# Hybrid decoder layer: token norms from the turned tokens by TensorE in place of loaded prompt rows, constant tables loaded in other places, page numbers read once per pair

## The reference, cut to what matters

```python
xn = rmsnorm(h, norm1)                       # h: (tokens, 1024), all f32
p = xn @ w_in                                # 3592 columns: q, k, v, conv inputs, z, gates
oa = diff_attention(q, k, v, paged cache)    # 4 heads
ob, state = gated_delta(conv(qkv_b), g, beta)
h = h + concat(norm(oa), norm(ob) * silu(z)) @ w_out
h = h + peer_ffn(rmsnorm(h, norm2))          # 128 of 16384 experts per token, gathered
rmsnorm(x, g) = x * rsqrt(mean(x * x) + 1e-6) * g
```

## Time and profile before

| | |
|---|---|
| median of 3 runs | 2050.31 us (2047.03 to 2055.94) |
| the profiled execution | 2046.96 us |
| its span, first to last instruction | 2045.1 us |
| TensorE busy | 1691.6 us (83%) |
| VectorE busy | 1335.3 us (65%) |
| ScalarE busy | 802.0 us (39%) |
| GpSimd busy | 785.1 us (38%) |
| moved by DMA | 758.91 MB, 371 GB/s over the span |

### The profile page before, as it was taken

The page is one execution under the profiler, slowest core; times in us unless marked ns, Lnnn a source line. Parts: engine busy times, 40 slices in busy tenths (PEclk is TensorE's granted clock), DMA queues, the critical chain, the costliest instruction groups (busy, mean ns, idle before and its releaser), DMA issues.

```text
span 2045.1 us, 20559 instructions
## 1 busy us (share of the span) xinstructions
PE 1691.6 (83%) x6211; PEld 853.0 (42%) x6211; DVE 1335.3 (65%) x3023; ACT 802.0 (39%) x2371; POOL 785.1 (38%) x670
## 2 busy tenths in 40 slices
PE   7697999988897878989787888978997657866777
PEld 2242464547453445445344544533563213522111
DVE  1344514344897657897665888775688967679544
ACT  1342322131645523563453346354344423333332
POOL 2111110111444444435444353534444555554442
PEclk9798999999999989999898999999999888987999
DMA  9999823226999999999999999999999999999997
GB/s 333 358 309 382 263 92 118 93 104 244 406 414 409 427 428 428 426 426 411 428 421 429 426 426 400 416 426 393 427 427 426 427 427 427 427 427 427 427 427 313
DMA packets 137015, 758.91 MB, mean 371 GB/s; under 512 B 15263, under 2 KB 24495, under 8 KB 60472
## 3 DMA queue, kind: packets, MB, share of 16 engines
q0 software_dynamic: 88448, 622.22, 73.4%
q1 hardware_dynamic: 44976, 128.07, 16.8%
q10 hardware_dynamic: 3480, 7.31, 1.0%
HBM read 741.56 MB, written 16.26 MB: 371 GB/s over the span
## 4 chain that ended last, share of the span: by engine, by line
PE 38%; DMA 30%; DVE 16%; ACT 7%; issue 4%; SPq 3%; POOL 2%; ACTq 0%; DVEq 0%; POOLq 0%
DMA sb_uv<-in_peer_uv,sb_eidx 27%; PE bank L2224 16%; PE bank L1827 8%; DVE sb_uv L1806 7%; PE bank L2151 3%; PE bank L2191 2%; DVE sb_hres L1780 2%; SPq L841 1%; POOL sb_uv L1006 1%; SPq L845 1%; ACT sb_diag L1384 1%; DMA sb_w<-in_w_sections 1%; PE bank L1941 1%; ACT sb_ew L1377 1%; PE bank L1953 1%
## 5 line engine op out<-in xcount | busy, mean ns | idle before, releaser
L2224 PE MATMUL bank<-sb_uv,sb_diag 128*128 128x512 f32 (+1 forms) x1860 | 943.2, 643 | 277.8 <-ACT sb_diag L1384 267.8
L1006 POOL DMA_INDIRECT sb_uv<-in_peer_uv,sb_eidx x576 | 704.1, 1222 | 829.8 <-PE bank L2224 646.4
L1806 DVE CUSTOM_DVE_ANT_0 sb_uv<-sb_uv,sb_xn 128x1024 f32<-128x1024 f32 x576 | 698.9, 1220 | 280.5 <-DMA sb_uv<-in_peer_uv,sb_eidx 277.6
L2224 PEld LDWEIGHTS bank<-sb_uv,sb_diag 128*128 128x128 f32 (+1 forms) x1860 | 333.8, 194 | 766.4 <-ACT sb_diag L1384 440.7
L1373 ACT ACTIVATE sb_gel<-sb_h 128x1 f32<-128x1 f32 x576 | 116.3, 202 | 753.5 <-DVE sb_h L1806 750.4
L1827 PE MATMUL bank<-sb_w,sb_xnT 128*128 128x512 f32 (+1 forms) x560 | 270.3, 626 | 24.7 <-DMA sb_w<-in_w_sections 11.7
L1384 ACT ACTIVATE sb_diag<-sb_stay,sb_ew 128x128 f32<-128x128 f32 (+1 forms) x465 | 183.2, 394 | 45.7 <-PE bank L2224 2.5
L1377 ACT ACTIVATE sb_ew<-sb_gel,sb_gate 128x1 f32<-128x1 f32 x576 | 169.7, 295 | 19.8
L1827 PEld LDWEIGHTS bank<-sb_w,sb_xnT 128*128 128x128 f32 (+1 forms) x560 | 100.6, 190 | 149.8 <-issue 122.6
L1780 DVE SCALAR_TENSOR_TENSOR sb_hres<-sb_uv,sb_ew,sb_hres 128x1024 f32<-128x1024 f32 x111 | 142.2, 1281 | 0.1
L2191 PEld LDWEIGHTS bank<-sb_rT,sb_zone 128*128 128x128 f32 x832 | 99.3, 193 | 15.7 <-issue 15.3
(11 more groups left out here) (352 smaller groups left out, 1593.2 us busy)
## 6 DMA issues: line engine op xcount, KB each, us to landing
sb_zone<-in_w_route SPq DMA_DIRECT2D x11, 2304.0 KB, 11.8
sb_w<-in_w_sections SPq DMA_DIRECT2D x40, 512.0 KB, 7.3
sb_zone<-in_w_mixer SPq DMA_DIRECT2D x8, 2048.0 KB, 15.6
sb_uv<-in_peer_uv,sb_eidx POOLq DMA_INDIRECT x576, 14.0
sb_sS<-in_cache_kT SPq DMA_DIRECT2D x32, 256.0 KB, 7.3
sb_zone<-in_cache_kT SPq DMA_DIRECT2D x32, 256.0 KB, 7.2
sb_held<-in_cache_v SPq DMA_DIRECT2D x32, 256.0 KB, 7.0
sb_zone<-in_cache_v SPq DMA_DIRECT2D x32, 256.0 KB, 5.9
```

Source lines behind the costliest of these rows:

```text
L1006: nc.gpsimd.indirect_dma_start(uv[:, m % RING, :], None, i["peer_uv"], bass.IndirectOffsetOnAxis(ap=eidx[:, t % 2, n:n + 1], axis=0)).then ...
L1806: nc.vector.tensor_tensor_reduce(out=uv[:, m % RING, 0:D], in0=uv[:, m % RING, 0:D], in1=xn2[:, t % 2, :], scale=1.0, scalar=0.0, op0=ALU. ...
L2224: ins = nc.tensor.matmul(bank[half][0:rows, :], lhsT=G["diag"][:, d % DIAGS, 0:rows], rhs=uv[:, m % RING, D + 512 * half:D + 512 * half + ...
```

## The change

Five things are done together.

1. The rows of the four prompt tiles are not loaded in the front. ScalarE squares the *turned* tokens of tiles 0 to 3 from `xnT` into the same borrowed buffers, without a sum. `square_sums(n)` lets TensorE sum over the features: eight matmuls of 128x128 squares with one column of -0.5, into column n of bank 7. `x_mean` reads that column. VectorE's gain multiply of a tile now waits for its square (`s_xsq`). Tile `PT` keeps its rows.
2. `SUMMED`, the due times of squares, sums, means and powers, goes from (20.5, 60, 66, 72, 77) to (20.5, 35, 50, 57, 65).
3. `s_tables` is split. `s_early` counts `w_ba` and the early table, now due at 49 in place of 54 and 59; `s_stay` counts the rest of the stay table, now due at 110 in place of 56, and `gain2T`, whose 4 KB load goes from GpSimd to SP.
4. The values of a pair use the page numbers that SP read for its keys.
5. Pieces 22 and 23 (the last two of the third conv section's first use) have a due time 4.5 earlier.

```diff
-SUMMED = (20.5, 60, 66, 72, 77)
+SUMMED = (20.5, 35, 50, 57, 65)
...
                 def x_loads():
-                    for n, t in enumerate(ORDER):
-                        yield early_at((1.0, 42, 48, 53, 58)[n])
-                        if t < PT:
-                            sp.dma_start(xin[n], i["x_prompt"][0, 128 * t:128 * t + 128, :]).then_inc(s_x[n], 16)
...
+                    yield early_at(1.0)
+                    sp.dma_start(xin[0][0:NSAMP], i["x_sample"].rearrange("b s d -> (b s) d")).then_inc(s_x, 16)
+                    sp.dma_start(xin[0][MROW:LAST], i["meta_tokens"]).then_inc(s_x, 16)
...
-                    yield early_at(54)
-                    sp.dma_start(F["wba"][:, :, :], i["w_ba"]).then_inc(s_tables, 16)
-                    yield early_at(56)
-                    sp.dma_start(stay[:, 128:], stay_table[:, 128:]).then_inc(s_tables, 16)
-                    yield early_at(59)
-                    sp.dma_start(F["early"][:, :], early_table).then_inc(s_tables, 16)
+                    yield early_at(49)
+                    sp.dma_start(F["wba"][:, :, :], i["w_ba"]).then_inc(s_early, 16)
+                    sp.dma_start(F["early"][:, :], early_table).then_inc(s_early, 16)
+                    yield early_at(110)
+                    sp.dma_start(stay[:, 128:], stay_table[:, 128:]).then_inc(s_stay, 16)
...
-                            yield unit_at(n) + 0.25 * used * unit_len(n)
+                            yield unit_at(n) + 0.25 * used * unit_len(n) - (4.5 if n == LAST_OF[4] and used < 3 else 0)
...
                 def value_loads(p):
...
-                            pages = []
-                            for g in range(4):
-                                n = (2 * p + seq) * NPG + 4 * half + g
-                                pages.append(sp.value_load(F["pages"][0:1, n:n + 1], min_val=0, max_val=i["cache_v"].shape[0] - 1))
+                            pages = pages_of[p, half, seq]
...
                 def x_squares(n):
...
+                    if n < 4:
+                        act.wait_ge(s_xTl[n], 16)
+                    else:
+                        act.wait_ge(s_ident, 48)
+                    nc.scalar.activation(xin[n].rearrange("p (k r) -> p k r", k=KC), xT(t), ACT.Square).then_inc(s_xsq, 1)
...
                 def xT_gains():
...
+                        if n:
+                            dve.wait_ge(s_xsq, n)
...
                 def x_mean(n):
...
+                    total, share = (F["ss"][0:rows, t:t + 1], 1.0 / D) if n == 0 else (bank[7][0:rows, n:n + 1], -2.0 / D)
+                    nc.vector.tensor_scalar(F["ms"][0:rows, t:t + 1], total, share, EPS, ALU.mult, ALU.add).then_inc(s_ms, 1)
...
+                def square_sums(n):
+                    yield early_at(SUMMED[n] + 0.3)
+                    if n == 1:
+                        pe.wait_ge(s_set, 1)
+                        pe.wait_ge(s_ss, 1)
+                    else:
+                        pe.wait_ge(s_ms, n)
+                    pe.wait_ge(s_xsq, n)
+                    for k in range(KC):
+                        ins = nc.tensor.matmul(bank[7][:, n:n + 1], lhsT=xin[n][:, 128 * k:128 * k + 128], rhs=minus_half[:, 0:1], start=k == 0, stop=k == KC - 1)
+                    ins.then_inc(s_ss, 1)
...
                 def small_columns():
...
-                    pe.wait_ge(s_tables, 48)
+                    pe.wait_ge(s_early, 32)
...
                 def decay_totals():
...
-                    pe.wait_ge(s_tables, 48)
+                    pe.wait_ge(s_stay, 16)
+                    pe.wait_ge(s_early, 32)
```

More of the change, by code:

```diff
@@ L369, in hybrid_step @@
         s_ident = sem("identity_and_gain1_loaded")
-        s_tables = sem("tables_loaded")
-        s_x = [sem(f"x_loaded{r}") for r in range(NT)]
+        s_early = sem("gate_columns_and_early_tables_loaded")
+        s_stay = sem("stay_tables_and_gain2_loaded")
+        s_x = sem("sample_rows_loaded")
+        s_xsq = sem("turned_tokens_squared")
         s_gain = sem("qk_gains_loaded")
@@ L2202, in queries @@
                     ins.then_inc(s_s2p, 1)
-                work = [Stream(unit(n)) for n in range(len(UNITS))] + [Stream(turn(u)) for u in range(2 * NT)] + [Stream(small_columns()), Stream(decay_totals())]
+                work = [Stream(unit(n)) for n in range(len(UNITS))] + [Stream(turn(u)) for u in range(2 * NT)] + [Stream(square_sums(n)) for n in range(1, NT)] + [Stream(small_columns()), Stream(decay_totals())]
                 work += [Stream(gdn(u)) for u in range(NT)] + [Stream(sample_updates(h)) for h in range(NH)]
```

33 lines of the change are left out of this document (16 added, 17 removed).

## The result

The changed kernel is slower: 2059.97 us median (2057.59 to 2067.25) against 2052.16 us (2047.03 to 2055.94) for the kernel before on the same chip, ratio 1.0044 with a 95% interval of 1.003 to 1.0058. By the ratio the change costs 9 us; I had predicted a gain of 9, 2041.3 us. The profiled execution took 2058.18 us, span 2056.4, which is 11.3 us over the span of 2045.1 before.

The account below looks back on a forecast made before the run. TensorE's queue was taken to bound 256 to 511 us, the gathers' DMA what follows. A lead of 8 us at unit 13's weights plus 1 us of clock gave 2050.3 - 9 = 2041.3 us, range 2030 to 2051.

Parts of the forecast that it names:

- What bounds the kernel: From 256 to 511 us TensorE's queue, busy 241.4 of 255 us; before, TensorE and DMA by turns; after, gathers' DMA.
- the 12.5 us wait: TensorE's wait ahead of the gate columns, put down to the early table, issued at 75.02; 12.5 us to be regained.
- Price of a sum: Each TensorE sum of 16 one-column records: 1.9 us (0 to 0.44 a record), 7.6 us in all.
- dear sums: Rival, 2054 us, chance 0.08: one-column records cost 0.44 each, adding 20.6 us ahead of the first key products.
- First and second sum: TensorE waits for squares, 5.3 us between units 1 and 2, 3.5 us between turns; first key products 16 us behind.
- Given back: From first key products to gate columns, waits and lower clock regained: 21.3 us, less 16 is 5.3 us ahead.
- Stay table: Issued at some 129, landing within 12.3 us; TensorE waits 2 us (0 to 6) at the totals, leaving 3 us ahead.
- Page numbers: 64 reads saved on SP, 38 us, some 9.6 a pair, so weight pieces 22 and 23 issue sooner.
- Weight pieces: At unit 13: pieces 22, 23 issued at some 162, 171, piece 23 landing at 187, TensorE 8 us ahead.
- Transfers decide: Rival, 2045 us, chance 0.16: DMA engines bound the front, only 2.1 MB or 5.5 us gained, sooner issue worth nothing.
- My last list: Signs that would show the forecast right or wrong, the wrong ones including sums above 3 us; no time or chance.
- the slower case I did price: The rival of one-column records costing 0.44 us each before the first key products: 2054 us, 3 us slower, chance 0.08.

Follow-up runs that it names:

- stay_early: The changed kernel with the rest of the stay table issued right behind the early table instead of at due time 110; 2050.55 us, ratio 1.0001.
- totals_later: The changed kernel, stay table left late, with the three steps using the decay totals placed 17.5 us later in their engines' orders; 2052.01 us, ratio 0.9998.
- softmax_first: sums_in_gaps with a pair's last softmax steps moved on VectorE ahead of the convolution multiply that waits for rows; 2035.88 us, ratio 0.9932.
- split_only: The kernel before with only the tables' part: early table due at 49, stay table at 110, count split; 2061.47 us, ratio 1.0056.
- rows_kept: The kernel before with both tables issued at 49 and the change's page numbers and weight pieces, rows still loaded and summed on ScalarE; 2047.06 us, ratio 0.9978.
- pages_pieces: The kernel before with only page numbers read once per pair and weight pieces 22 and 23 asked for sooner; 2050.58 us, ratio 0.9993.
- sums_in_gaps: stay_early with ScalarE's squares and TensorE's sums given due times of their own, each sum later than its square; 2038.16 us, ratio 0.9926.
- gaps_stay_late: sums_in_gaps with the stay table back at due time 110, so the changed kernel with only squares and sums moved; 2047.47 us, ratio 0.9987.
- quarter_rows: rows_kept with only the first quarter of each prompt row loaded and squared, so it computes other values; 2042.31 us, ratio 0.9953.
- stay_between: softmax_first with the stay table due at 92 and the steps on the totals 17.5 us later; 2036.26 us, ratio 0.992.

## Why the prediction was wrong, by its steps

I forecast 9 us less and got 9 more. Of these 18 us, 9 are the stay table's wait, which stay_early and totals_later give back; the other 9 are the gain that I expected from the weights of unit 13 and that the rest of the change does not have.

*What bounds the kernel.* The releaser of the 12.5 us wait was read rightly: with the early table sooner the wait is gone in every run. "TensorE's queue is the bound, and a lead or lag there passes on one to one" was said of the stretch from 256 us. There it holds for the change (10.9 us at `kb`, 10.9 at the first gather, 11.3 at the end), less so for softmax_first (5.7 at `kb`, 3.0 at the first gather). My sum went on as if a lead of TensorE near 200 us were a lead at 256, and it isn't. Of the leads at the gate columns (14 us in split_only and rows_kept) 2.3 us at most reached `kb`, and of that at unit 14 (8.8 us in pages_pieces) nothing, since `kb` is VectorE's, behind convolution multiplies that wait for rows through DMA. The lead of sums_in_gaps arrived whole. By the traces it is there before the prompt tiles' convolution units begin (unit 4 at 45.20, against 56.66 in the changed kernel), so their rows can come sooner with it.

*Price of a sum.* 1.9 us was right for TensorE at the upper clock: 1.84 us for 16 records, 0.115 each, at a granted clock of 1.00. At 0.50 it is 3.41 to 3.55, 0.21 to 0.22 each; the second, at 0.82, took 2.25. The four took 11.05 us in place of 7.6. The *dear sums* rival (0.44 a record) is out.

*First and second sum.* Predicted waits 5.3 and 3.5, measured 6.60 and 3.82. Up to the end of unit 3 the sum was right (50.2 predicted, 33.59 + 16.29 = 49.9 measured). First key products predicted at 71.1, measured at 75.05: the three sums behind unit 3 took 7.5 us in place of 5.7, and the 20 records of unit 4 between them 13.8 (3.70, 8.18 and 1.96) in place of 10.8, because the granted clock, for which I had given 2 us, was 0.50 from 56.66 to 63.6 and 0.65 from there to 71.45. I took the place of the sums as given, and did not price it. It is the larger part of the story: later, where the squares are ready, the same sums cost 8.9 us (3 x 1.84 and 3.41) and no wait, and the time falls by 12 to 15 us.

*Given back.* 21.3 predicted. From the first key products (75.05) to the end of the gate columns (some 92.1, four groups at 1.03 us as I said) it took 17.1 us where 38.8 stood before: 21.7. The predicted lead of 5.3 us was 1.9 at the products behind (93.87 against 95.78); the 4 us by which the first key products came late account for the difference.

*Stay table.* **This is the step that failed.** I had it issued at 129 and landed in 12.3 us with a wait of 2 (0 to 6). It was issued at 136.94, landed in 15.9, and the wait was 9.0, though TensorE asked only at 143.9 (152.94 less 9.02) and not at 135.4. The size was off by 7 us, and the path was wrong: I priced the wait by its length on TensorE, and did not ask what ScalarE and VectorE had queued behind the same data. They are the 18.4 us and the 8.9 us above. That the loss came out as long as TensorE's wait, 9 us each, is chance: TensorE had caught up by unit 14, and in gaps_stay_late a wait of 8.3 us goes with 12 us. stay_early and totals_later both give back 9 us, the one by moving the load, the other by moving the users.

*Page numbers.* The saving is real: the 2.4 us gap in SP's queue between the value loads is gone (143.96 + 6.14, then 150.20). The rival that gives it no worth had 16%, and pages_pieces shows its time, 0.9993. The Trainium skill, "DMA: Bandwidth & Descriptors", section "Issuing engines are not separate DMA queues", cited there, says that issuing from several engines saves only the time that the issues take. The measured time agrees. The way to it is another: at a DMA share of 1.04 from 120 to 204 us the sooner issue did bring the weights sooner (waits of 1.1 us in place of 11.7, unit 14 8.8 us sooner), and this was lost behind VectorE's multiplies.

*Weight pieces.* Piece 22 was issued at 179.32, not 162, and 23 at 188.78, not 171; even so TensorE's wait fell to 0.5, as TensorE itself was late. "8 us ahead" did not come there. It did in pages_pieces (169.43 and 179.57, 8.8 us ahead at unit 14) and was worth nothing, with `kb` 0.6 us later than before: **the second step that failed**, since nothing in the prediction followed the gain past unit 13.

*Rivals.* *Transfers decide* gave 5.5 us for 2.1 MB. quarter_rows does not bear that out in the front, where three quarters of the bytes gave 1.5 us at `kb`; what the removed rows give with their sums well placed is 11 us (rows_kept against sums_in_gaps), most of it not by their bytes. My last list named the sign that came: "a wait over 5 us at the totals, or a wait for conv data that takes the lead away between 204 and 256 us". It had no price and stood in no rival; the slower case I did price was another mechanism.

## What to carry to other kernels

- A wait is priced by what is queued behind it on every engine that uses the same data, not by its length on the engine one looks at: on TensorE 9.0 us cost 9, 8.3 cost 12, and 9.7 removed gave nothing. If a load must be late, its users can be placed later: here that gave back as much (9 us) as an early load.
- Before a removed wait is booked as a gain, follow it to the next place where the engines meet, and see who releases that one. Here the traces show VectorE, behind multiplies waiting for rows.
- A cheap added step costs what its place makes it cost. The same four sums were worth 12 to 15 us more where their squares were ready.

## What was not expected of the hardware

- A one-column fp32 record with 128x128 weights takes 0.115 us on TensorE at a granted clock of 1.00 (16 in 1.84 us) and 0.213 at 0.50 (16 in 3.41 us); a 64-column one with the same weights takes 0.118 at 1.00 (16 in 1.89 us). From 1 to 64 columns 16 records grow by 0.05 us, from one clock level to the other by 1.57.
- Removing 1.6 MB of loads from a front with a DMA share of 0.88 to 1.04 brought its end 1.5 us nearer, where the bytes by themselves take 4 us at 384 GB/s (an estimate); moving 0.8 MB out of the front of it (stay_between) gave nothing at its end.
